# Routed expert weights asked for in ten parts, two in flight, in place of three whole matrices

## What is computed

```python
# x: (1, 2048, 1024); w_gate, w_up: (1, 64, 1024, 256); w_down: (1, 64, 256, 1024)
h = layernorm(ALPHA * x + mixer(x))
scores = sigmoid(h @ w_router)             # 64 experts, 8 chosen for each token, in groups
# the 16384 pairs (token, expert) are sorted by expert and cut into blocks of 128 rows
for toks, weight, e in blocks:             # a block has one expert
    xb = h[toks]
    yb = (silu(xb @ w_gate[e]) * (xb @ w_up[e])) @ w_down[e]
    acc[toks] += yb * weight
out = layernorm(ALPHA * h + acc + shared_expert(h))
```

## Time and profile before

| what | value |
|---|---|
| median of three runs | 2489.15 us |
| profiled execution | 2485.66 us, of which the span is 2483.8 us |
| TensorE busy | 2382.5 us (96%) |
| VectorE, ScalarE, GpSimd busy | 1575.5, 1161.9, 767.3 us |
| moved by DMA | 524.34 MB, mean 211 GB/s |
| routed experts, 1000 to 2200 us | DMA engines busy 0.86, granted clock 1.00 |

### The profile page before, as it was taken

The page is one execution under the profiler, slowest core; times in us unless marked ns, Lnnn a source line. Parts: engine busy times, 40 slices in busy tenths (PEclk is TensorE's granted clock), DMA queues, the critical chain, the costliest instruction groups (busy, mean ns, idle before and its releaser), DMA issues. The chain is left out here.

```text
span 2483.8 us, 49979 instructions
## 1 busy us (share of the span) xinstructions
PE 2382.5 (96%) x11840; PEld 1954.7 (79%) x11842; DVE 1575.5 (63%) x2285; ACT 1161.9 (47%) x1621; POOL 767.3 (31%) x829
## 2 busy tenths in 40 slices
PE   8899999989997799999999999999999999999986
PEld 6677777678886688888888888888888888888875
DVE  6686867768878756555665555656665556655447
ACT  4525253542225645445554445545554445544334
POOL 0010100011110134334543433534443334444327
PEclk9999999989998899999999999999999999999998
DMA  7242323364445579778988878888888789987863
GB/s 254 77 144 98 111 94 111 117 218 164 171 164 206 196 230 284 223 219 270 273 259 233 254 218 263 268 266 262 257 253 243 224 223 274 283 247 222 216 221 136
DMA packets 253808, 524.34 MB, mean 211 GB/s; under 512 B 18065, under 2 KB 165169, under 8 KB 249649
## 3 DMA queue, kind: packets, MB, share of 16 engines
q1 hardware_dynamic: 204464, 336.64, 39.7%
q0 software_dynamic: 48672, 186.86, 29.4%
q10 hardware_dynamic: 608, 0.02, 0.0%
HBM read 386.61 MB, written 136.87 MB: 211 GB/s over the span
## 5 line engine op out<-in xcount | busy, mean ns | idle before, releaser
L2503 PE MATMUL psG<-gu_split,xT_hi 128*128 x2624 | 624.3, 390 | 2.9 <-ACT xT_hi L2340 1.5
L2503 PEld LDWEIGHTS psG<-gu_split,xT_hi 128*128 128x128 f32 x2624 | 493.8, 188 | 106.2 <-issue 3.6
L2326 POOL DMA_INDIRECT acc<-y,si x162 | 290.1, 1791 | 728.6 <-DMA acc<-y,si 413.3
L2409 DVE TENSOR_TENSOR gu_split<-raw_gu,gu_split (+1 forms) x127 | 290.6, 2288 | 175.3 <-ACT gu_split L2344 171.7
L2514 PE MATMUL psG<-gu_split,xT_lo 128*128 x1304 | 339.3, 402 | 5.9 <-issue 5.8
L2514 PEld LDWEIGHTS psG<-gu_split,xT_lo 128*128 128x128 f32 x1304 | 233.1, 188 | 50.1 <-issue 8.7
L2344 ACT ACTIVATE gu_split<-raw_gu x126 | 234.3, 1907 | 33.5 <-issue 33.5
L2301 POOL DMA_INDIRECT xg<-htab,gi x164 | 205.0, 1250 | 130.4 <-POOL gi L2298 109.7
L2409 DVE TENSOR_TENSOR d_lo<-raw_d,d_hi (+1 forms) x64 | 146.7, 2292 | 149.5 <-ACT d_hi L2344 149.5
L2389 ACT ACTIVATE HT_hi<-psH 128x256 fp32r<-128x256 f32 x162 | 62.4, 385 | 351.6 <-PE psH L2521 351.6
L2406 DVE TENSOR_TENSOR xT_lo<-psX,xT_hi 128x512 fp32r<-128x512 f32 x328 | 209.7, 680 | 8.5 <-ACT xT_hi L2340 8.5
(11 more groups left out here) (388 smaller groups left out, 3723.7 us busy)
## 6 DMA issues: line engine op xcount, KB each, us to landing
raw_gu<-in_w_gate_dram SPq DMA_DIRECT2D x64, 1024.0 KB, 6.0
raw_gu<-in_w_up_dram SPq DMA_DIRECT2D x64, 1024.0 KB
raw_d<-in_w_down_dram SPq DMA_DIRECT2D x64, 1024.0 KB, 6.9
wring<-split_d SPq DMA_DIRECT2D x24, 1024.0 KB, 4.8
split_d<-wring POOLq DMA_DIRECT2D x8, 1024.0 KB, 4.2
raw_d<-mixed SPq DMA_DIRECT2D x16, 512.0 KB, 3.9
xt<-in_x_dram SPq DMA_DIRECT2D x16, 512.0 KB, 4.3
htab<-h SPq DMA_DIRECT2D x16, 512.0 KB, 2.6
```

What stands on the lines that cost most here:

```text
L2326: nc.gpsimd.indirect_dma_start(out=acc, out_offset=bass.IndirectOffsetOnAxis(ap=si[k][:, 0:1], axis=0), in_=y[k][:], in_offset=None, compu ...
L2409: nc.vector.tensor_tensor(dst, src, hi, ALU.subtract).then_inc(dlo_s if n == 2 else gulo_s, 1)
L2503: nc.tensor.matmul(psG[slot][:], xT_hi[slot][:, c, :], right[:, bass.ds(w, 1), c, :].rearrange("p a n -> p (a n)"), start=(n == 0 and c == ...
```

## The change

Each 1 MB of gate and of up becomes four transfers of 256 KB, two 128-row pieces of the matrix each, and down becomes two transfers of 512 KB. Each of the three semaphores becomes a pair: even parts count on one, odd parts on the other. In the loop of `experts` SyncE keeps a list of the two parts last asked for, and before it asks for a part it waits until the part two ahead of it has landed. This runs on over the seams: up's first part waits for gate's third, down's first for up's third, and the next expert's first gate part for this expert's first down part. The waits on `gulo_s` and `dlo_s` stay, once for each matrix. The first two experts are also loaded in parts, but their ten transfers are issued back to back. ScalarE waits on both semaphores of a pair where it waited on one. The shared expert's loads are as before.

```diff
-                        sp.wait_ge(sm, e * 16)
-                        carry_wait(sp, passed)
-                        sp.dma_start(dst, w[0, bass.ds(e, 1)].rearrange("a (k p) n -> p (a k) n", p=P)).then_inc(sm, 16)
+                        n = D_PARTS if sm is down_in else GU_PARTS
+                        for q, (to, rows) in enumerate(weight_parts(w[0, bass.ds(e, 1)], dst, sm is down_in, by_run=False)):
+                            last, of, load, part = ahead.pop(0)
+                            sp.wait_ge(last[q % 2], load * (16 * of // 2) + 16 * (part // 2 + 1))
+                            carry_wait(sp, passed)
+                            sp.dma_start(to, rows).then_inc(sm[q % 2], 16)
+                            ahead.append((sm, n, e, q))
...
+def weight_parts(w, dst, down, by_run=False):
+
+    n = D_PARTS if down else GU_PARTS
+    each = (FE // P if down else KC) // n
+    rows = w.rearrange("a (p k) n -> p (a k) n" if by_run and not down else "a (k p) n -> p (a k) n", p=P)
+    for q in range(n):
+        at = slice(q * each, (q + 1) * each)
+        yield dst[:, at, :], rows[:, at, :]
...
             def split_gate_up(entry, before):
 
                 e = entry.next()
-                act.wait_ge(gate_in, e * 16 + 16)
-                act.wait_ge(up_in, e * 16 + 16)
+                for p in range(2):
+                    act.wait_ge(gate_in[p], (e + 1) * (16 * GU_PARTS // 2))
+                    act.wait_ge(up_in[p], (e + 1) * (16 * GU_PARTS // 2))
...
             def split_down(entry, before):
                 e = entry.next()
-                act.wait_ge(down_in, e * 16 + 16)
+                for p in range(2):
+                    act.wait_ge(down_in[p], (e + 1) * (16 * D_PARTS // 2))
```

More of the change, by code:

```diff
@@ L41 @@
 HT_AHEAD = 6
+GU_PARTS, D_PARTS = 4, 2
 TURN = 2
@@ L1858, in _ @@
                     act.wait_ge(disp_s, TILES)
-                    act.wait_ge(loaded[0], 16)
-                    act.wait_ge(loaded[1], 16)
+                    for w in range(2):
+                        for p in range(2):
+                            act.wait_ge(loaded[w][p], 16 * GU_PARTS // 2)
                     for at in halves:
@@ L2128, in _, with load_expert @@
                     down(n)
-def load_expert(eng, w_gate, w_up, w_down, expert, slot, wgu, wd, loaded):
-    for w, sm, dst in zip((w_gate, w_up, w_down), loaded, (wgu[:, slot, :, 0:FE], wgu[:, slot, :, FE:], wd[:, slot])):
-        eng.dma_start(dst, w[0, expert].rearrange("(k p) n -> p k n", p=P)).then_inc(sm, 16)
+def weight_parts(w, dst, down, by_run=False):
[5 more added lines that the diff above has]
+        yield dst[:, at, :], rows[:, at, :]
+def load_expert(eng, w_gate, w_up, w_down, expert, slot, wgu, wd, loaded, in_parts=False):
+    gate, up = wgu[:, slot, :, 0:FE], wgu[:, slot, :, FE:]
+    for w, sm, dst in zip((w_gate, w_up, w_down), loaded, (gate, up, wd[:, slot])):
+        if in_parts:
+            for q, (to, rows) in enumerate(weight_parts(w[0, expert:expert + 1], dst, w is w_down, by_run=False)):
+                eng.dma_start(to, rows).then_inc(sm[q % 2], 16)
+        else:
+            eng.dma_start(dst, w[0, expert].rearrange("(k p) n -> p k n", p=P)).then_inc(sm, 16)
 def experts(nc, passed, w_gate, w_up, w_down, ident, htab, acc, table, n_turns, idx, xg, gi, gi_s, x_in, acc_out, gu, guhi_s, gulo_s, wgu, wd, loaded, y, si, added,
@@ L2272, in _ @@
                     before = sp.value_load(table[0:1, bass.ds(e + WORDS, 1)], min_val=0, max_val=EXPERTS)
+                    ahead = [(down_in, D_PARTS, e - 1, q) for q in range(D_PARTS - 2, D_PARTS)]
                     for w, sm, dst in ((w_gate, gate_in, wgu[:, s, :, 0:FE]), (w_up, up_in, wgu[:, s, :, FE:]),
@@ L2291, in _ @@
                 prefetch(sp)
-            for sm in (gate_in, up_in, down_in):
-                sp.wait_ge(sm, 16 * EXPERTS)
+            for sm, parts_ in ((gate_in, GU_PARTS), (up_in, GU_PARTS), (down_in, D_PARTS)):
+                for p in range(2):
+                    sp.wait_ge(sm[p], 16 * parts_ // 2 * EXPERTS)
         @block.gpsimd
@@ L2347, in _ @@
             block0, block1 = entries(act, 0, 2)
-            act.wait_ge(down_in, 16)
+            for p in range(2):
+                act.wait_ge(down_in[p], 16 * D_PARTS // 2)
             pieces = list(parts(0, 1))
@@ L3030, in decoder_layer @@
               w_out, raw_gu, raw_d, wo_hi, wo_lo, shared, early)
-        loaded = [ctx.enter_context(nc.semaphore(n)) for n in ("gate_in", "up_in", "down_in")]
+        loaded = [[ctx.enter_context(nc.semaphore(f"{n}{p}")) for p in range(2)] for n in ("gate_in", "up_in", "down_in")]
         shared_in = ctx.enter_context(nc.semaphore("shared_in"))
@@ L3059, in prefetch_first @@
         def prefetch_first(eng):
-            load_expert(eng, w_gate, w_up, w_down, 0, 0, raw_gu, raw_d, loaded)
+            load_expert(eng, w_gate, w_up, w_down, 0, 0, raw_gu, raw_d, loaded, in_parts=True)
         def prefetch_second(eng):
-            for sm in loaded:
-                eng.wait_ge(sm, 16)
-            load_expert(eng, w_gate, w_up, w_down, 1, 1, raw_gu, raw_d, loaded)
+            for sm, n in zip(loaded, (GU_PARTS, GU_PARTS, D_PARTS)):
+                for p in range(2):
+                    eng.wait_ge(sm[p], 16 * n // 2)
+            load_expert(eng, w_gate, w_up, w_down, 1, 1, raw_gu, raw_d, loaded, in_parts=True)
         place_in = ctx.enter_context(nc.semaphore("place_in"))
```

## The result

| | before | changed |
|---|---|---|
| median of six runs each | 2488.93 us (2487.29 to 2493.26) | 2522.65 us (2515.98 to 2543.89) |
| ratio, 95% interval | | 1.0146 [1.0109, 1.0183] |
| profiled execution, span | 2485.66, 2483.8 us | 2530.36, 2528.5 us |
| routed experts, first to last transpose of `xg` | 1531.2 us | 1572.2 us |

A forecast was written before the change was run, and what follows sets the result against it. TensorE was taken as the bound, busy 2382.5 of 2483.8 us. From 2485.66, -4 for shorter waits and +2 for late loads gave 2483.7, plus 3.5 to the median: 2487 us; 8 in 10 between 2479 and 2520.

The forecast's parts named there:

- What bounds the kernel, and the room of a load: Routed experts: TensorE busy 1194.96 of 1200 us; gate and up have 28.9 us to land, 18.55 in runs, 23.1 on average.
- A link in the clear, 3.45 us: SyncE's chain of weight parts, landing to landing: 3.2 us transfer plus 0.24 us wait and issue, two parts side by side.
- So half of the 3.7 us hides: GpSimd's scatter and gather take 3.7 us of the engines per block; half was to hide in the chain's own gaps.
- T = 22 us: SyncE's time per expert load: T = 18.0 / (1 - 1.85 / 9.28) = 22.5 us, taken as 22, under the mean 23.1.
- A spare of 12 us: Gate and up were to be through after 17 us of their 28.9, leaving 12 us.
- +2 us in all: Charge for late loads in three known runs of two-block experts, not all as long: +2 us, range 0 to +12.
- a second rival at 0.16: Loads fall back in the runs: at T = 23, about +8 us in each of three runs, 2511 us; chance 0.16.
- What comes back: Scatters wait behind fewer weight rows, so gathers and TensorE's turn starts at line 2514 wait less: -4 us.
- The rest at nothing: ScalarE's added semaphore waits and `prefetch_first`'s seven extra transfers cost nothing; 2.7 us once if the latter's cover were gone.
- The chain as the bound: Rival: SyncE's chain becomes the bound, decided at T = 23.1 us; at 25 us, +106 us, 2593 us; chance 0.12.
- Gathers did not suffer: Rival judged: gathers suffer everywhere as the weights' queue is never empty, +35 us less the 4, about 2518; chance 0.05.
- Scatters did not wait as before: Rival judged: scatters wait as before beside the weight loads, neither gain nor loss, 2489 us; chance 0.12.

## Why the prediction was wrong, point by point

**What bounds the kernel, and the room of a load.** Right. 28.9 us for a load, 18.55 in a run and 23.1 over all are what the stall of 1258 us is made of.

**A link in the clear, 3.45 us.** Right as far as the runs tell: without scatters four links took 13.9 us on average, forecast 13.8. Gathers still ran beside them, so a link with nothing beside it may be shorter.

**"So half of the 3.7 us hides", T = 22 us.** This is the step that failed. In the run the chain took 23.9 us a load. Put into the prediction's own formula, 23.9 = 18.0 / (1 - x / 9.28) gives x = 2.3 us of the 3.7 that do not hide, in place of 1.85, and the prediction had then rounded 22.5 down to 22. The run without scatters agrees: four links grew from 13.9 to 18.1 us with the scatters, 4.2 us in 18.1 / (1572.2 / 162) = 1.9 blocks, so about 2.2 us a block did not hide. More than half of the 3.7 us shows in the chain, which the prediction had named as a sign that it is wrong. Over the stretch the mean from first gate part to first gate part was 23.94; less the 49.2 / 61 = 0.8 us in which SyncE waited for gate and up slots, the chain took 23.1 us a load. That is the mean interval of before, so there was no margin left: SyncE made up its lateness only where several experts of three blocks followed each other, and the stalls fell between these places.

**A spare of 12 us.** Also too large. For the load followed above, gate and up were through 21.5 us after the request, not 17, which left 7.6. The prediction counted 17 us to the end of the fourth link; the loads took 18.1 us on average to down's first issue (17.2 in the first one shown, 1182.36 - 1165.20, and 20.3 in the one followed), and there the last part of up is still in flight.

**"Three such runs", "+2 us in all".** The mechanism was named, a second rival at 0.16: loads fall back, the split waits, `y` is copied late behind it, TensorE stands. Its price of 8 us a run is near what was found: against two parts of 512 KB, which have the same limit and the same waits at a turn's start gone, the stretch is 49.7 us longer for six stalls, 8.3 each. What was wrong is the number of stalls, six against three. The runs are three, as the prediction says: gate's requests of before have three runs of six short intervals (18.5 to 20.3 us), from 1161.9, 1516.3 and 2050.0 us. In the changed kernel the first two gave one stall each and the third gave two. The other two stalls fall among three pairs of short intervals, with a single expert of three blocks between one pair and the next, where the chain can't catch up. The first stall also came at the fourth load of its run, not at the last. 2511 with six in place of three would have been 2535. And the +2 us was too low even at T = 22: 5 us too late, less the 2 that ScalarE hides, is 3 us for each of three runs, all six intervals long, 9 us in all. The parts of the price were also not those that I had. "ScalarE can hide perhaps 2 us" was about right (9.56 became 6.97), but the lower clock behind each stall had no term: 1534.62 - 1519.43 = 15.2 of the 49.7 us.

**What comes back, "-4 us".** The gain is real and larger, hidden under the loss: the stretch is 8.7 us shorter with two parts of 512 KB, and TensorE's waits at a turn's start went from 5.8 us to 0.3. "TensorE can gain no more than 5.8 + 1.5 us" was a little low; its busy time fell too, from 1522.31 to 1519.43. The reason given for it stands only in part. It was that no more than 32 rows stand ahead of a scatter on each engine, but without a limit, with as many rows asked for as before, most of the gain is there. The longest wait of GpSimd for a scatter's landing was 8.0 us before, 7.5 with whole matrices and the limit, and 6.4 to 7.2 with parts of 256 or 512 KB.

The landings themselves can be worked out from the traces, from a scatter's issue to the last recorded count of its semaphore, for all scatters up to the last load of the loop. Of scatters issued from 4 us ahead to 3 us behind a load's first gate transfer the median was 10.5 us before and 8.1 in the changed kernel, forecast 7 to 8; of all others it was 6.5 and 7.5. Landings of over 10 us fell from 38 of 149 to 4 of 148, and the longest near a load was 10.8 us, where none of 11 was forecast. Without the limit they fell as well, to 8 of 146 with 256 KB and 6 of 147 with 512 KB, while with whole matrices and the limit they stayed at 39 of 147. So smaller transfers cut the long landings and make the others somewhat longer. That this is what freed TensorE at a turn's start is argued, not shown.

**The rest at nothing.** Right as far as it shows: apart from the stretch of the experts and the 3.0 us ahead of it, 0.7 of the 44.7 us are left.

**The other rivals.** The chain as the bound is decided at T = 23.1 us, and the chain was just there; parts of 128 KB show that rival past the point. Gathers did not suffer: the waits at a turn's start, where a late gather would show, are gone. The prediction's 2518 us for that rival is also 4 us too low, since the 2487 us to which it adds 35 has the -4 in it already. Scatters did not wait as before: every kernel in parts lost most of the waits at a turn's start and most of the landings of over 10 us. On the packet-by-packet turns of the Trainium skill ("DMA: Bandwidth & Descriptors", queues, rings and completion order) the time would have stayed the same when only the transfers' size changed; here the stretch fell by 6.2 to 6.5 us with the size alone, so the measurement decides against the rival that followed from it, which says nothing yet on how the engines turn.

The rule of at least 1 MiB per DMA on the same page of the Trainium skill, in its rules for kernel authors, warned in the right direction, but what the runs show is not about the DMA's size alone. At two in flight, 128 KB, 256 KB, 512 KB and 1 MB gave 1.156, 1.015, 0.996 and 0.999, and at 256 KB with four in flight 0.997.

**Left open.** Whether two parts of 512 KB and four of 256 KB differ at all (0.9956 and 0.9967, intervals that overlap). The run without scatters is a single one, and it changes what GpSimd waits for as well as the traffic. And whether ScalarE could start gate's split while up is in flight: it waits for both ahead of the first; this was not tried.

## What to carry to other kernels

A chain in which each transfer waits for an earlier one has a pace of its own. Work out that pace with the other queues' traffic beside it, and hold it against the shortest stretch of compute that it must feed, then against the mean: between the two it gives stalls in runs of short stretches, and a following run starts late if the longer stretches between are too few, so go through the whole profile interval by interval to count them; above the mean it is the bound. When a limit on transfers in flight is wanted, choose the bytes in flight (here 1 MB was enough and 512 KB was not) and then the size. Price a stall on TensorE with the clock that it loses, not by its idle time alone.

## What the runs showed of the hardware

A stall of 7 us on TensorE was followed by a granted clock of 0.63 over 6 us, with pairs of matmuls at 1.05 us in place of 0.62; over six stalls this was nearly half as much again as the idle time. A transfer of half the bytes did not halve a link: 3.1 us at 128 KB against 4.5 at 256 KB, with scatters beside both, and 3.5 at 256 KB without scatters. And transfers of 256 or 512 KB in place of 1 MB, as many bytes asked for at once, took 6 us off a stretch in which the DMA engines were busy 0.85 of the time before and 0.85 to 0.86 after, and brought the scatters that took over 10 us to land from 38 of 149 to 8 of 146 and 6 of 147.
